# The output projection of a hybrid decoder block as seven quarter products

## The chip, the cores and the metric

The kernel runs on one core of one Trainium2 chip. The metric is the device time of one execution in microseconds.

## What is computed

One decoder layer on 512 tokens of width 1024. Cut to what matters here:

```python
merged = jax.nn.sigmoid(gate_a) * (ya @ w_branch_a[l]) + jax.nn.sigmoid(gate_b) * (yb @ w_branch_b[l])
h = h + merged @ w_out[l]                 # the output projection: 512x1024 by 1024x1024
xn2 = rms_norm(h, norm2_w[l])
h = h + (jax.nn.silu(xn2 @ w_ffn_gate[l]) * (xn2 @ w_ffn_up[l])) @ w_ffn_down[l]
```

## The kernel before, in words

Every product is formed from operands that are split in two: a high part (rounded to the matmul type by ScalarE, `w_hi`, `A_hi`, `mg_hi`) and the low rest (`x - high`, formed by VectorE or GpSimd, `w_lo`, `A_lo`, `mg_lo`). Each tile product is three matmuls: high by high, high by low, low by high.

The five engines run programs written out by hand, and semaphores order them; there is no scheduler. The stages in order of time: the input projection, the gated attention and gating unit, the *merge* (gates and branches, seven *pairs* of weight blocks), the output projection, the feed-forward *pairs* (gate and up) and the down projection.

In the merge and the feed-forward a pair is computed by a seven-product scheme for 2x2 blocks (Strassen-Winograd). With weight quarters A11, A12, A21, A22 the left operands are A11, A12, A22 and the sums S1 = A21 + A22, S2 = S1 - A11, S3 = A11 - A21, S4 = A12 - S2. The right operands are quarters of the activations and the differences T1 = x12 - x11, T2 = x22 - T1, T3 = x22 - x12, T4 = x21 - T2. Seven products of a quarter each give what eight plain ones would. There the weight sums lie in PSUM (`chain` in banks 4 and 5, `diff` in banks 6 and 7), and the products are collected in banks 0 to 3 (`product`, L2104).

The output projection before does not use this. `W_out` arrives in four blocks of two 128-row slices by 1024 columns (1 MB each, SyncE, L394 and L398). ScalarE rounds each (`out_high`, `high2`), VectorE (`low_out`, the first) or GpSimd (`low_out`, `low`) forms its low part. `block_N` (L1899) then runs, for each block, over four row tiles t, two halves of 512 columns and two slices k: 3 matmuls of 512 columns each, 48 in a block, 192 in all, with the merged rows as the stationary operand. The eight sums (4 row tiles, 2 halves) fill all eight PSUM banks. In the last block, while row tiles 2 and 3 are multiplied, row tiles 0 and 1 of h already go through `residual` (VectorE), `stats_h` and `normalise_h` (ScalarE) and are turned on TensorE (`turn`, 8 transposes) for the feed-forward.

What is merged is formed during and just after merge pair 7: GpSimd multiplies the branch products by the gates (`weighted(7)`, L508, two instructions, after the last quarter `merge_c12` of pair 7), VectorE adds the branches (`merged_sum(u)`, L1529, u = 0 to 3), ScalarE rounds (`merged_high`, L914), VectorE subtracts (`merged_low`, L1542).

## Time and profile before

| what | value |
|---|---|
| median of 3 runs | 817.0 us (816.84 to 817.6) |
| span of the profiled execution | 815.2 us |
| TensorE busy (matmul) | 808.4 us, 99% |
| VectorE, ScalarE, GpSimd busy | 539.7, 440.4, 414.0 us |
| from the last matmul of merge pair 7 to the first of the feed-forward | 424.7 to 470.3 us |

Of the profiled execution the profile gives the span, from the first to the last instruction; it has no further time of its own. "PE" is TensorE, "PEld" its weight load, "DVE" VectorE, "ACT" ScalarE, "POOL" GpSimd, "SP" SyncE. A duration behind a time is that of one instruction, or of x so many from the start of the first to the end of the last. Durations of instructions in a row overlap by a few hundredths, since the next starts while the last one drains.

### The profile page before, as it was taken

To read this page: it belongs to the slowest core of one execution; us is meant where nothing else is said; L and a number is where in the kernel's file an instruction comes from. 1 tells how busy PE (TensorE), PEld (TensorE's weight loads), DVE (VectorE), ACT (ScalarE), POOL (GpSimd) and SP (SyncE) were. 2 spreads that over 40 slices of the span, in tenths; PEclk is the share of its full clock that TensorE was granted. 3 is DMA by queue.
4 is the path that set the end of the run, shared out by engine and by line. 5 is a ranking of instruction groups with operands and counts; after the bars stand their busy time and mean duration, and the time that the engine had idled before them with its cause. 6 is when DMAs were issued, how large, how long until landed. Compare 5 with 4: busy or idle time off the path is not lost.

```text
span 815.2 us, 13365 instructions
## 1 busy us (share of the span) xinstructions
PE 808.4 (99%) x5504; PEld 750.1 (92%) x5504; DVE 539.7 (66%) x561; ACT 440.4 (54%) x501; POOL 414.0 (51%) x146
## 2 busy tenths in 40 slices
PE   9999999999999999999999999999999999999997
PEld 7888888888888899999998899999999999999985
DVE  5377377374674867888873278766667777677736
ACT  5523446665665645866542584454444446665624
POOL 4445424424224543477954543544444445978880
PEclk9999999999999999999999999999999999999999
DMA  7973523121123253322234203423234445535022
GB/s 294 265 263 115 164 95 104 52 104 57 52 98 115 95 204 105 104 104 105 103 130 185 104 1 107 152 106 109 106 111 159 159 152 186 178 125 212 1 78 104
DMA packets 27565, 103.11 MB, mean 126 GB/s; under 512 B 2816, under 2 KB 4224, under 8 KB 23552
## 3 DMA queue, kind: packets, MB, share of 16 engines
q1 hardware_dynamic: 22288, 87.07, 29.8%
q10 hardware_dynamic: 5232, 15.40, 5.9%
q8 instruction: 33, 0.54, 0.3%
...
## 4 chain that ended last, share of the span: by engine, by line
PE 99%; DMA 0%; ACT 0%; issue 0%; SPq 0%; DVE 0%; ACTq 0%
PE acc L2109 14%; PE acc L2112 14%; PE acc L2111 14%; PE acc L1894 7%; PE acc L1896 6%; PE acc L1895 6%; PE acc L1913 6%; PE acc L1912 6%; PE acc L1911 6%; PE acc L2308 3%; PE acc L2307 3%; PE acc L2305 3%; PE acc L1940 3%; PE acc L2023 1%; PE acc L2062 1%; PE acc L2067 1%
## 5 line engine op out<-in xcount | busy, mean ns | idle before, releaser
L465 POOL TENSOR_TENSOR w_lo<-raw,w_hi 128x2048 fp32r<-128x2048 f32 x26 | 123.1, 4733 | 163.1 <-ACT w_hi L660 163.1
L486 POOL TENSOR_TENSOR A_lo<-wp,A_hi 128x1024 fp32r<-128x1024 f32 x51 | 126.1, 2472 | 145.6 <-ACT A_hi L833 137.3
L848 ACT ACTIVATE S_hi<-acc 128x1024 fp32r<-128x1024 f32 x68 | 68.1, 1024 | 89.5 <-PE acc L2112 56.3
L2112 PE MATMUL acc<-xt_hi,A_lo 128*128 128x256 f32 x408 | 115.5, 283 | 0.0
L2111 PE MATMUL acc<-xt_lo,A_hi 128*128 128x256 f32 x408 | 115.5, 283 | 0.0
L2109 PE MATMUL acc<-xt_hi,A_hi 128*128 128x256 f32 x408 | 115.5, 283 | 0.0
L1444 DVE TENSOR_TENSOR S_lo<-acc,S_hi 128x1024 fp32r<-128x1024 f32 x68 | 81.8, 1220 | 18.6 <-ACT S_hi L848 18.6
L1894 PE MATMUL acc<-xt_hi,w_hi 128*128 128x512 f32 (+1 forms) x240 | 92.5, 385 | 0.0
L1896 PE MATMUL acc<-xt_hi,w_lo 128*128 128x512 f32 (+1 forms) x240 | 91.7, 382 | 0.0
L1895 PE MATMUL acc<-xt_lo,w_hi 128*128 128x512 f32 (+1 forms) x240 | 91.7, 382 | 0.0
L660 ACT ACTIVATE w_hi<-raw 128x2048 fp32r<-128x2048 f32 x26 | 49.5, 1909 | 64.1 <-PE acc L1913 43.3
L2111 PEld LDWEIGHTS acc<-xt_lo,A_hi 128*128 128x128 f32 x408 | 78.3, 192 | 0.0
L2109 PEld LDWEIGHTS acc<-xt_hi,A_hi 128*128 128x128 f32 x408 | 78.3, 192 | 0.0
L2112 PEld LDWEIGHTS acc<-xt_hi,A_lo 128*128 128x128 f32 x408 | 78.3, 192 | 0.0
L2109 PE MATMUL acc<-tb_hi,S_hi 128*128 128x256 f32 x240 | 67.9, 283 | 0.0
L2111 PE MATMUL acc<-tb_lo,S_hi 128*128 128x256 f32 x240 | 67.9, 283 | 0.0
L2112 PE MATMUL acc<-tb_hi,S_lo 128*128 128x256 f32 x240 | 67.9, 283 | 0.0
L833 ACT ACTIVATE A_hi<-wp 128x1024 fp32r<-128x1024 f32 x51 | 53.8, 1055 | 17.9 <-PE acc L2112 17.9
L1896 PEld LDWEIGHTS acc<-xt_hi,w_lo 128*128 128x128 f32 x240 | 45.1, 188 | 8.8
L1894 PEld LDWEIGHTS acc<-xt_hi,w_hi 128*128 128x128 f32 x240 | 45.1, 188 | 8.8
L1895 PEld LDWEIGHTS acc<-xt_lo,w_hi 128*128 128x128 f32 x240 | 45.1, 188 | 8.5
L2109 PE MATMUL acc<-mt_hi,S_hi 128*128 128x256 f32 x168 | 47.7, 284 | 0.0
...
## 6 DMA issues: line engine op xcount, KB each, us to landing
wp<-wstream SPq DMA_DIRECT2D x34, 1024.0 KB, 6.9
raw<-wstream SPq DMA_DIRECT2D x26, 1024.0 KB, 4.8
...
raw_out<-wstream SPq DMA_DIRECT2D x2, 1024.0 KB, 5.8
```

The lines of the kernel that those rows point to most:

```text
L465: pool.tensor_tensor(w_lo[s][:, :], raw[s][:, :], w_hi[s][:, :], ALU.subtract).then_inc(lo_ready, 1)
L486: pool.tensor_tensor(low_of(name, rows), weights_of(name, c, rows), high_of(name, rows), ALU.subtract).then_inc(plain_low, 1)
L660: a.activation(w_hi[s][:, :], raw[s][:, :], ACT.Copy).then_inc(hi_ready, 1)
L833: a.activation(high_of(name, rows), weights_of(name, c, rows), ACT.Copy).then_inc(op_high, 1)
L848: a.activation(high_of(name, rows), src, ACT.Copy).then_inc(op_high, 1)
L1444: v.tensor_tensor(low_of(name, rows), src, high_of(name, rows), ALU.subtract).then_inc(s_low, 1)
L1894: pe.matmul(dst, wh[:, k, cs], rh[:, k, ts], start=(k == 0), stop=False)
L1895: pe.matmul(dst, wh[:, k, cs], rl[:, k, ts], start=False, stop=False)
L1896: last = pe.matmul(dst, wl[:, k, cs], rh[:, k, ts], start=False, stop=(k == KD - 1))
L2109: pe.matmul(dst, wh[:, g, k, :], x[0][:, k, :], start=(start and g == 0 and k == 0), stop=False, skip_group_check=True)
L2111: pe.matmul(dst, wh[:, g, k, :], x[1][:, k, :], start=False, stop=False, skip_group_check=True)
L2112: mm = pe.matmul(dst, wl[:, g, k, :], x[0][:, k, :], start=False, stop=(k == 3), skip_group_check=True)
```

## The change

The output projection is computed by the same seven-product scheme, with quarters of 512 by 512 weights. A quarter product (`out_product`) runs over two row tiles and four slices with 3 matmuls of 512 columns: 24 matmuls, 168 in the seven. The merged rows (and their differences `mgt`, formed by VectorE) are the stationary operand. `W_out` comes in eight transfers of half a quarter (512 KB). The weight sums (`out_chain`, and S3 in the place of A21) lie in SBUF, because all eight banks hold products: A11 and A12 in 4 and 5, S1 and S4 in 6 and 7, S2 in 0 and 1, S3 and A22 in 2 and 3. What several quarters share goes through `out_u2` and `out_u3`; GpSimd adds it to three quarters of h (`based`), VectorE adds the rest from the banks (`residual`). Some semaphores elsewhere are joined into one; no other stage changes. Here and below "S1's low" is the low part of that operand.

```diff
-        raw_out = [sb(f"raw_out{s}", 120 + 16 * s, [P, BLK]) for s in range(2)]
-        raw_ffn = [sb(f"raw_ffn{s}", 181 + 8 * s, [P, BLK]) for s in range(2)]
+        out_raw = {n: sb(f"out_raw_{n}", kb, [P, 4, HALF]) for n, kb in (("A11", 112), ("A21", 120), ("A12", 128), ("A22", 136))}
+        out_chain = sb("out_chain", 32, [P, 4, HALF])
+        OUT_SLOT = {"A11": (16, 24), "S1": (0, 8), "S2": (181, 189), "S3": (16, 24), "A12": (0, 8), "A22": (181, 189), "S4": (197, 40)}
+        out_hi = {n: sb(f"out_{n}_hi", kb[0], [P, 4, HALF], F32R) for n, kb in OUT_SLOT.items()}
+        out_lo = {n: sb(f"out_{n}_lo", kb[1], [P, 4, HALF], F32R) for n, kb in OUT_SLOT.items()}
+        mgt = [sb(f"mgt{n}", 160 + 4 * n, [P, 4, HT]) for n in range(4)]
+        out_u2 = sb("out_u2", 104, [P, 2, HALF])
...
-            sp.wait_ge(t_formed, N_FORMED)
-            for s in range(2):
-                sp.dma_start(raw_out[s][:, :], wstream[W_OUT + s]).then_inc(raw_landed[s], 16)
-            sp.wait_ge(hi_ready, B_OUT + 2)
...
+            sp.wait_ge(t_low, N_LOW)
+            for name, landed in out_landed.items():
+                i, j = int(name[1]) - 1, int(name[2]) - 1
+                for n in range(2):
+                    sp.dma_start(out_raw[name][:, 2 * n:2 * n + 2, :],
+                                 wstream[W_OUT + 2 * j + n].rearrange("p (k n) -> p k n", k=2)[:, :, i * HALF:(i + 1) * HALF]
+                                 ).then_inc(landed, 16)
+            sp.wait_ge(out_low_pool, 1)
+            sp.wait_ge(out_formed, 3)
+            sp.dma_start(raw_ffn[0][:, :], wstream[W_FFN]).then_inc(ffn_landed[0], 16)
+            sp.wait_ge(out_low, 3)
+            sp.dma_start(raw_ffn[1][:, :], wstream[W_FFN + 1]).then_inc(ffn_landed[1], 16)
+            sp.wait_ge(out_done, 10)
...
-            low_out(1)
...
+            def based(n, ts, hs, u):
+                pool.wait_ge(out_joined, n)
+                pool.tensor_tensor(h[:, ts, hs], h[:, ts, hs], u[:, :, :], ALU.add).then_inc(h_based, 1)
+            out_low_of("A11", 1)
             weighted(MERGE_PAIRS)
-            for b in range(B_OUT + 2, B_FFN):
-                low(b, b % 2, 8 * (b - b % 2) + 16)
+            pool.wait_ge(mg_high, 4)
+            pool.tensor_tensor(xt_lo[:, 4:8, 0:HT], sg_a[:, 4:8, 0:HT], xt_hi[:, 4:8, 0:HT], ALU.subtract).then_inc(mg_low_pool, 1)
+            pool.wait_ge(mg_high, 5)
+            pool.tensor_tensor(mt_lo[2][:, :, :], mgt[2][:, :, :], mt_hi[2][:, :, :], ALU.subtract).then_inc(mg_low_pool, 1)
+            out_low_of("A12", 5)
+            pool.wait_ge(h_landed, 16)
+            based(2, slice(2, 4), slice(HALF, D), out_u3)
+            based(1, slice(0, 2), slice(HALF, D), out_u2)
+            based(1, slice(2, 4), slice(0, HALF), out_u2)
...
+            pool.wait_ge(out_low, 5)
             ffn_low(0)
...
+                if p == MERGE_PAIRS:
+                    a.wait_ge(plain_low, 3 * p - 3)
+                    a.wait_ge(s_formed, 4 * p - 4)
+                    out_high_of("A11", out_raw["A11"])
...
+                    merged_high(xt_hi[:, 0:4, 0:HT], sg_a[:, 0:4, 0:HT], msum=2)
...
+                    merged_high(mt_hi[0][:, :, :], mgt[0][:, :, :], formed=1)
...
-            a.wait_ge(product_done, 7 * MERGE_PAIRS)
-            a.dma_start(h[:, :, :], x.rearrange("(t p) n -> p t n", p=P)).then_inc(h_landed, 16)
+            a.wait_ge(plain_low, 3 * MERGE_PAIRS)
+            a.wait_ge(s_formed, 4 * MERGE_PAIRS)
+            out_high_of("S1", out_chain, 1)
+            a.wait_ge(product_done, 7 * MERGE_PAIRS - 1)
+            out_high_of("S2", out_chain, 2)
             a.wait_ge(joined, 5 * MERGE_PAIRS)
             a.dma_start(ident[:, :], ident_d).then_inc(ident_landed, 16)
-            merged_high(2)
-            merged_high(3)
+            a.wait_ge(out_done, 2)
+            a.wait_ge(branch_taken, 8)
+            a.activation(out_u2[:, :, :], acc[:, 4:6, :], ACT.Copy).then_inc(out_taken, 1)
+            out_high_of("S3", out_raw["A21"], 3)
+            merged_high(mt_hi[1][:, :, :], mgt[1][:, :, :], formed=2)
+            merged_high(xt_hi[:, 4:8, 0:HT], sg_a[:, 4:8, 0:HT], msum=4)
+            merged_high(mt_hi[2][:, :, :], mgt[2][:, :, :], formed=3)
+            a.wait_ge(out_done, 4)
+            out_high_of("A12", out_raw["A12"])
+            merged_high(xt_hi[:, 0:4, HT:SEQ], mgt[3][:, :, :], formed=4)
+            merged_high(xt_hi[:, 4:8, HT:SEQ], sg_a[:, 4:8, HT:SEQ], msum=4)
+            a.wait_ge(out_done, 6)
+            a.dma_start(h[:, :, :], x.rearrange("(t p) n -> p t n", p=P)).then_inc(h_landed, 16)
+            out_high_of("A22", out_raw["A22"])
+            out_high_of("S4", out_chain, 4)
...
-            for j in range(2):
-                high2(B_OUT + 2 + j, j % 2, block_used, 6 + j + 1)
-            a.wait_ge(block_used, 6 + 3)
+            a.wait_ge(out_done, 8)
             ffn_high(0)
+            ffn_high(1)
...
                     merged_sum(1)
-                    merged_low(0)
-                    low_out()
+                    v.wait_ge(msum_ready, 2)
+                    mgt_form(0, m12, m11)
+                    merged_low(xt_lo[:, 0:4, 0:HT], m11, xt_hi[:, 0:4, 0:HT], 1)
+                    v.wait_ge(out_landed["A21"], OUT_LANDED)
+                    v.wait_ge(out_landed["A22"], OUT_LANDED)
+                    v.tensor_tensor(out_chain[:, :, :], out_raw["A21"][:, :, :], out_raw["A22"][:, :, :], ALU.add).then_inc(out_formed, 1)
+                    merged_low(mt_lo[0][:, :, :], mgt[0][:, :, :], mt_hi[0][:, :, :], 2)
...
             merge_c12(MERGE_PAIRS)
-            merged_low(1)
-            for u in (2, 3):
-                merged_sum(u)
-                merged_low(u)
...
+            out_low_of("S1", out_chain, 2)
+            v.wait_ge(out_low, 1)
+            v.tensor_tensor(out_chain[:, :, :], out_chain[:, :, :], out_raw["A11"][:, :, :], ALU.subtract).then_inc(out_formed, 1)
+            v.tensor_tensor(out_raw["A21"][:, :, :], out_raw["A11"][:, :, :], out_raw["A21"][:, :, :], ALU.subtract).then_inc(out_formed, 1)
+            merged_sum(2)
+            out_low_of("S2", out_chain, 3)
+            merged_sum(3)
+            v.wait_ge(msum_ready, 4)
+            mgt_form(1, m22, mgt[0][:, :, :])
+            mgt_form(2, m22, m12)
+            merged_low(mt_lo[1][:, :, :], mgt[1][:, :, :], mt_hi[1][:, :, :], 3)
+            out_low_of("S3", out_raw["A21"], 4)
+            v.wait_ge(mgt_formed, 2)
+            mgt_form(3, m21, mgt[1][:, :, :])
+            v.wait_ge(out_low, 2)
+            v.wait_ge(out_landed["A12"], OUT_LANDED)
+            v.tensor_tensor(out_chain[:, :, :], out_raw["A12"][:, :, :], out_chain[:, :, :], ALU.subtract).then_inc(out_formed, 1)
+            merged_low(xt_lo[:, 0:4, HT:SEQ], mgt[3][:, :, :], xt_hi[:, 0:4, HT:SEQ], 6)
+            merged_low(xt_lo[:, 4:8, HT:SEQ], m22, xt_hi[:, 4:8, HT:SEQ], 7)
+            v.wait_ge(out_done, 6)
+            v.wait_ge(out_taken, 1)
+            v.tensor_tensor(out_u2[:, :, :], acc[:, 0:2, :], out_u2[:, :, :], ALU.add).then_inc(out_joined, 1)
+            out_low_of("A22", out_raw["A22"], 6)
+            v.wait_ge(out_done, 8)
+            v.wait_ge(out_joined, 1)
+            v.tensor_tensor(out_u3[:, :, :], acc[:, 2:4, :], out_u2[:, :, :], ALU.add).then_inc(out_joined, 1)
+            out_low_of("S4", out_chain, 7)
+            def residual(t, hf, b, done):
+                v.wait_ge(out_done, done)
+                hs = h[:, t, hf * HALF:(hf + 1) * HALF]
+                v.tensor_tensor(hs, bank[b][:, :], hs, ALU.add).then_inc(h_joined, 1)
             v.wait_ge(h_landed, 16)
+            residual(0, 0, 4, 9)
+            residual(1, 0, 5, 10)
+            v.wait_ge(h_based, 1)
+            residual(2, 1, 6, 4)
+            residual(3, 1, 7, 4)
+            v.wait_ge(h_based, 2)
...
-            residual(0, 16)
+            residual(0, 1, 2, 11)
             rstd_h(0)
-            residual(1, 16)
+            residual(1, 1, 3, 12)
             rstd_h(1)
             weigh_turned(0)
-            residual(2, 16)
...
-                block_N(j % 2, mg_hi[:, ks, :], mg_lo[:, ks, :], j == 0, j == 3, quarters_taken, turn_h)
...
+            def out_product(name, x, b, start, between=None):
+                wh, wl = out_hi[name], out_lo[name]
+                for t in range(2):
+                    dst = bank[b + t][:, :]
+                    ts = slice(t * P, (t + 1) * P)
+                    for k in range(4):
+                        pe.matmul(dst, x[0][:, k, ts], wh[:, k, :], start=(start and k == 0), stop=False, skip_group_check=True)
+                        pe.matmul(dst, x[0][:, k, ts], wl[:, k, :], start=False, stop=False, skip_group_check=True)
+                        mm = pe.matmul(dst, x[1][:, k, ts], wh[:, k, :], start=False, stop=(k == 3), skip_group_check=True)
+                        if between is not None and k == 1:
+                            between(t)
+                    mm.then_inc(out_done, 1)
+            pe.wait_ge(out_low_pool, 1)
+            pe.wait_ge(mg_low, 1)
+            out_product("A11", x11, 4, True)
+            pe.wait_ge(out_low, 1)
+            pe.wait_ge(mg_low, 2)
+            out_product("S1", mt1, 6, True)
+            pe.wait_ge(taken, 2 * MERGE_PAIRS)
+            pe.wait_ge(joined, 5 * MERGE_PAIRS)
+            pe.wait_ge(out_low, 2)
+            pe.wait_ge(mg_low, 3)
+            out_product("S2", mt2, 0, True)
+            pe.wait_ge(out_low, 3)
+            pe.wait_ge(mg_low_pool, 2)
+            out_product("S3", mt3, 2, True)
+            pe.wait_ge(out_taken, 1)
+            pe.wait_ge(out_low_pool, 2)
+            out_product("A12", x21, 4, False)
+            pe.wait_ge(out_low, 4)
+            pe.wait_ge(mg_low, 4)
+            pe.wait_ge(out_joined, 2)
+            out_product("A22", t4, 2, False)
+            def turn_h(t):
+                turn(hn[:, t, :], 2 * t, t)
+            pe.wait_ge(out_low, 5)
+            pe.wait_ge(mg_low, 5)
+            pe.wait_ge(h_joined, 4)
+            pe.wait_ge(ident_landed, 32)
+            out_product("S4", x22, 6, False, turn_h)
```

On VectorE, before, from the last two quarters of merge pair 7 on (`sg_a`, `sg_b` hold the two gated branches, `mcq` the quarters of the pair, `mg` the merged rows, `w_lo0` the first block's low part; brackets name semaphores waited for):

```order
L1535 TENSOR_TENSOR w_lo0_53<-raw_out0_112,w_hi0_51 128x2048 [waits product_done,hi_ready]
L1507 TENSOR_TENSOR mcq_72<-acc,mu2_74 128x512 [waits product_done] x2
L1542 TENSOR_TENSOR mg_lo_94<-sg_a_97,mg_hi_93 128x1024 [waits mg_hi_ready]
L1529 TENSOR_TENSOR sg_a_97<-sg_a_97,sg_b_98 128x1024 [waits branch_taken]
L1542 TENSOR_TENSOR mg_lo_94<-sg_a_97,mg_hi_93 128x1024 [waits lo_ready,mg_hi_ready]
```

and with the change, from the same two quarters to the low part of T2 (`mt_lo1`), the last operand that product S2 waits for:

```order
L1544 TENSOR_TENSOR mcq_72<-acc,mu2_74 128x512 [waits product_done] x2
L1579 TENSOR_TENSOR out_S1_lo_123<-out_chain_114,out_S1_hi_116 128x2048 [waits out_high]
L1647 TENSOR_TENSOR out_chain_114<-out_chain_114,out_raw_A11_110 128x2048 [waits out_low]
L1648 TENSOR_TENSOR out_raw_A21_111<-out_raw_A11_110,out_raw_A21_111 128x2048
L1566 TENSOR_TENSOR sg_a_95<-sg_a_95,sg_b_96 128x1024 [waits branch_taken]
L1579 TENSOR_TENSOR out_S2_lo_124<-out_chain_114,out_S2_hi_117 128x2048 [waits out_high]
L1566 TENSOR_TENSOR sg_a_95<-sg_a_95,sg_b_96 128x1024 [waits branch_taken]
L1571 TENSOR_TENSOR mgt1_130<-sg_a_95,mgt0_129 128x1024 [waits msum_ready]
L1571 TENSOR_TENSOR mgt2_131<-sg_a_95 128x1024
L1575 TENSOR_TENSOR mt_lo1_69<-mgt1_130,mt_hi1_66 128x1024 [waits mg_high]
```

Before, one low part (L1542) stood between the last quarter and the second block of weights. Now nine instructions stand between the last quarter and product S2, and all of them read two operands in SBUF.

On GpSimd, before, from the low part of A22 of merge pair 7 on:

```order
L486 TENSOR_TENSOR A_lo<-wp_127,A_hi 128x1024 [waits op_high]
L608 TENSOR_TENSOR w_lo_54<-raw_out_113,w_hi_52 128x2048 [waits hi_ready,lo_ready,product_done]
L508 TENSOR_TENSOR sg_b<-mcq,sg_b 128x1024 [waits joined,taken,tile_free,gates_taken]
L508 TENSOR_TENSOR sg_b<-mcq,sg_b 128x1024
L465 TENSOR_TENSOR w_lo_53<-raw_49,w_hi_51 128x2048 [waits hi_ready,raw_landed0]
```

and with the change:

```order
L498 TENSOR_TENSOR A_lo<-wp_148,A_hi 128x1024 [waits op_high]
L620 TENSOR_TENSOR out_A_lo<-out_raw_A_110,out_A_hi 128x2048 [waits out_high]
L520 TENSOR_TENSOR sg_b<-mcq,sg_b 128x1024 [waits joined,taken,tile_free,gates_taken]
L520 TENSOR_TENSOR sg_b<-mcq,sg_b 128x1024
L631 TENSOR_TENSOR xt_lo<-sg_a,xt_hi 128x4x256 [waits mg_high]
L633 TENSOR_TENSOR mt_lo_70<-mgt_131,mt_hi_67 128x1024 [waits mg_high]
L620 TENSOR_TENSOR out_A_lo<-out_raw_A_112,out_A_hi 128x2048 [waits out_high]
L626 TENSOR_TENSOR h<-h,out_u_134 128x2x512 [waits out_joined,h_landed]
L626 TENSOR_TENSOR h<-h,out_u_133 128x2x512 [waits out_joined] x2
L642 TENSOR_TENSOR w_lo_53<-raw_ffn_135,w_hi_51 128x2048 [waits hi_ready,out_low]
```

The low part of A11 no longer waits for VectorE and the pair's fifth product (`lo_ready`, `product_done`), so it runs right behind A22's; and three additions into h are new.

## Rows read from the trace of the kernel before

**Rows 1.** The page: busy time, and the chain that ended last by engine

```profile
PE 808.4 (99%) x5504; PEld 750.1 (92%) x5504; DVE 539.7 (66%) x561; ACT 440.4 (54%) x501; POOL 414.0 (51%) x146
...
PE 99%; DMA 0%; ACT 0%; issue 0%; SPq 0%; DVE 0%; ACTq 0%
```

**Rows 2.** Windows: merge pair 7, the output projection (PEclk: granted clock, 1.00 full)

```profile
core 0: us, PE busy (x) PEld busy (x) DVE busy (x) ACT busy (x) POOL busy (x), PEclk, DMA share, GB/s
404.60:424.70 20.10, 20.10 (x170) 20.10 (x169) 14.34 (x14) 10.02 (x10) 11.01 (x5) 1.00 0.34 130
424.70:470.30 45.60, 45.60 (x212) 37.92 (x212) 17.90 (x19) 16.81 (x21) 25.20 (x8) 1.00 0.41 156
```

**Rows 3.** Chain of waits (start us, us, what), and the turns in the last block

```profile
424.94 0.23 PE acc L1911
...
464.41 0.87 PE acc L1883 x8
...
468.03 0.87 PE acc L1883 x8
...
470.29 3.83 PE acc L2211 x32
```

**Rows 4.** Timeline of VectorE (start us, us, what, idle before), 414 to 435 us

```profile
414.52 1.22 DVE L1444 TENSOR_TENSOR S_lo<-acc,S_hi 128x1024 fp32r<-128x1024 f32 x1 [0.37 <-ACT S_hi L848]
415.66 1.22 DVE L1529 TENSOR_TENSOR sg_a<-sg_a,sg_b 128x1024 f32<-128x1024 f32 x1
416.79 0.68 DVE L1504 TENSOR_TENSOR u<-acc,mu 128x512 f32<-128x512 f32 x1
...
420.45 2.28 DVE L1535 TENSOR_TENSOR w_lo<-raw_out,w_hi 128x2048 fp32r<-128x2048 f32 x1
...
424.98 0.69 DVE L1507 TENSOR_TENSOR mcq<-acc,mu 128x512 f32<-128x512 f32 x1 [1.64 <-PE acc L2112]
425.59 3.33 DVE L1542 TENSOR_TENSOR mg_lo<-sg_a,mg_hi 128x1024 fp32r<-128x1024 f32 x1
431.20 3.41 DVE L1529 TENSOR_TENSOR sg_a<-sg_a,sg_b 128x1024 f32<-128x1024 f32 x1 [2.28 <-POOL sg_b L508]
```

**Rows 5.** Timeline of GpSimd over the same stretch

```profile
412.04 2.41 POOL L486 TENSOR_TENSOR A_lo<-wp,A_hi 128x1024 fp32r<-128x1024 f32 x1
423.23 4.61 POOL L608 TENSOR_TENSOR w_lo<-raw_out,w_hi 128x2048 fp32r<-128x2048 f32 x1 [8.78 <-DVE w_lo L1535]
427.80 5.72 POOL L508 TENSOR_TENSOR sg_b<-mcq,sg_b 128x1024 f32<-128x1024 f32 x2
```

**Rows 6.** Timelines of both engines from 371 us

```profile
371.79 3.02 DVE L1487 TENSOR_TENSOR yb<-yb,rt_b 128x1024 f32<-128x1024 f32 x1 [2.05 <-POOL xt_lo L512]
...
375.34 1.21 DVE L1444 TENSOR_TENSOR S_lo<-acc,S_hi 128x1024 fp32r<-128x1024 f32 x1
...
371.33 2.40 POOL L486 TENSOR_TENSOR A_lo<-wp,A_hi 128x1024 fp32r<-128x1024 f32 x1
373.69 5.77 POOL L508 TENSOR_TENSOR sg_a<-mcq,sg_a 128x1024 f32<-128x1024 f32 x2
```

**Rows 7.** Timelines of both engines from 266 us

```profile
269.35 5.73 DVE L1420 TENSOR_TENSOR yb<-yb,rs 128x512 f32<-128x512 f32 x2
...
266.95 7.58 POOL L481 TENSOR_TENSOR mt_lo<-mt_raw,mt_hi 128x1024 fp32r<-128x1024 f32 x3 [4.57 <-ACT mt_hi L824]
```

**Rows 8.** Timeline of ScalarE from 414 us

```profile
414.38 1.90 ACT L918 ACTIVATE w_hi<-raw_out 128x2048 fp32r<-128x2048 f32 x1
...
434.64 1.06 ACT L914 ACTIVATE mg_hi<-sg_a 128x1024 fp32r<-128x1024 f32 x1 [13.44 <-DVE sg_a L1529]
```

**Rows 9.** DMA issues (KB each, us to landing), 395 to 460 us, and SyncE's first issue

```profile
raw_out<-wstream SPq DMA_DIRECT2D x2, 1024.0 KB, 5.8
...
h<-x ACTq DMA_DIRECT2D x1, 2048.0 KB, 13.6
...
400.91 0.82 SPq L394 DMA_DIRECT2D raw_out<-wstream  x2
```

**Rows 10.** Timelines of VectorE and ScalarE: row tile 0 of h to its normalised rows

```profile
460.36 0.69 DVE L1613 TENSOR_TENSOR h<-acc,h 128x512 f32<-128x512 f32 x1 [0.60 <-PE acc L1913]
...
461.09 1.06 ACT L673 ACTIVATE sq_junk<-h 128x1024 f32<-128x1024 f32 x1
...
462.80 1.34 ACT L1000 ACTIVATE hn<-h,small 128x512 f32<-128x512 f32 x2 [0.23 <-DVE small L1619]
```

**Rows 11.** Groups by line, shapes apart: the one wait of TensorE over 0.4 us

```profile
L1930 PE MATMUL acc<-ones_dv 128*128 128x128 f32 x20 | 4.1, 386 | 1.2 <-DVE ones_dv L1203 1.2
```

More of the change, by code:

```diff
@@ L256, in build @@
         hi_ready, lo_ready, block_used = sem("hi_ready"), sem("lo_ready"), sem("block_used")
-        x_landed = [sem(f"x_landed{t}") for t in range(TT)]
+        rows_landed = [sem(f"rows_landed{t}") for t in range(TT)]
         xt_landed = [None] + [sem(f"xt_landed{q}") for q in range(1, 4)]
@@ L1619, in rstd_h @@
                 v.reciprocal(rstd[:, t:t + 1], sd[:, t:t + 1]).then_inc(rstd_ready, 1)
-            residual(0, 16)
+            residual(0, 1, 2, 11)
             rstd_h(0)
-            residual(1, 16)
+            residual(1, 1, 3, 12)
             rstd_h(1)
             weigh_turned(0)
-            residual(2, 16)
+            v.wait_ge(h_based, 3)
+            residual(2, 0, 6, 13)
             weigh_turned(1)
@@ L1629, in _ @@
             rstd_h(2)
-            residual(3, 16)
+            residual(3, 0, 7, 14)
             rstd_h(3)
```

193 lines of the change are left out of this document (81 added, 112 removed).

## The prediction

> **What bounds the kernel now.** I read the page first, then the windows, then the timelines of the three helper engines around the output projection. TensorE is busy for 99% of the span and makes 99% of the chain that ended last [rows 1]. So a matmul that goes away gains its time, and a wait that comes in costs its whole length. In the windows TensorE has no gap in merge pair 7 (20.10 us) nor in the output projection (45.60 us), and VectorE is busy for 17.90, GpSimd for 25.20 us of the latter [rows 2]. What the reader is to look for in the timelines is when each operand becomes ready, and how long VectorE and GpSimd take when both work at once.
>
> **What is removed.** From the first matmul of the old stage to the feed-forward it is 45.60 us [rows 2], and two turns of 0.87 us are in it [rows 3]. That leaves 43.86 us for 192 matmuls, 0.228 us each (the chain shows 0.23). The new stage has 168 of the same form: one quarter product takes 24 x 0.228 = 5.48 us, and the gain before any wait is the same 24 matmuls, **-5.5 us**.
>
> **The price of a helper's instruction.** On VectorE 1024 elements take 1.22 us and 2048 take 2.28 us [rows 4]; on GpSimd 2.41 and 4.61 us [rows 5]; on ScalarE 1.06 and 1.90 us [rows 8]. That holds when an engine works alone. At 425.59 VectorE's low part, both inputs in SBUF, took 3.33 us and ended at 428.92, which is 1.08 us behind the end of GpSimd's L608 (423.23 + 4.61 = 427.84). At 431.20 it took 3.41 us and ended at 434.61, again 1.09 us behind GpSimd (427.80 + 5.72 = 433.52). GpSimd in its turn took 5.72 us for two where twice 2.41 is 4.82 [rows 4, 5]. The same earlier: VectorE ends at 374.81, 1.08 us behind GpSimd's 373.73, and the next two on GpSimd take 5.77 us. But its low part with an input in PSUM (L1444, 375.34) takes 1.21 us in the midst of them [rows 6]. So an instruction of VectorE with both inputs in SBUF and one of GpSimd never run together: the one that asks later waits for the other's end. Two instructions of VectorE with little work took 5.73 us against three of GpSimd (7.58 us) [rows 7]: when both have more to do, they take turns. The old weight sums lie in PSUM and escape this. The new ones do not.
>
> No row shows an instruction of 2048 elements on VectorE waiting so. Below, it could overlap in part; above, it could pay 2.28 behind GpSimd's end. I take 2.14, from 2.28 less the 0.14 by which 1.08 is below 1.22. The Trainium skill ("SBUF — State Buffer", section "Who interferes with whom") says that a VectorE instruction with two SBUF inputs and a GpSimd one that reads SBUF exclude each other for the whole instruction; it names no size, and by that rule the sum below stands as it is.
>
> **The new chain, step by step** (times are those of the old trace, carried on; TensorE leaves merge pair 7 at 424.78).
>
> 1. *Merge pair 7.* GpSimd forms A11's low part right behind A22's, 414.4 to 419.0. `merged_sum(0)`, asked for at 415.66 [rows 4], ends at 420.05 instead of 416.88. u3, one quarter, `merged_sum(1)` and T1 follow, to 423.6, then the low part of x11, to 424.76. Product A11 can start at 424.8: no wait, but the margin is gone. The cover of all this was VectorE's idle time in pair 7 (5.8 of 20.1 us [rows 2]).
> 2. *S1.* The sum A21 + A22 to 426.95, T1's low to 428.1, two quarters to 429.3 (the last one at 425.7 before [rows 4]), S1's low to 431.5. Product A11 ends at 430.3. **Wait 1.2 us.**
> 3. *S2.* Behind S1's low VectorE and GpSimd take turns: GpSimd's first gated product to 433.7, S2's sum to 435.9, the second gated product to 438.15, S3's sum to 440.3. Then VectorE alone: merged sum 441.4, S2's low 443.6, merged sum 444.7, T2 446.0, T3 447.1, T2's low 448.3. Product S1 ends at 437.0. **Wait 11.4 us.** It is the largest term: nine instructions of VectorE from 429.2 on (four of 2.28 and five of 1.22, 15.2 us), and 4.5 us of GpSimd between them, less 0.6 that neighbours overlap, is 19.1 us to 448.3, against two products of 5.48.
> 4. *S3.* S3's low waits for x21's low on GpSimd (to 450.6) and ends at 452.7; then T3's low on GpSimd, to 455.0. Product S2 ends at 453.8. **Wait 1.2 us.**
> 5. *A12.* GpSimd's low part, behind T4 on VectorE, ends at 460.55; product S3 at 460.5. **Wait 0.1 us.**
> 6. *A22.* VectorE, behind that: S4's sum 462.7, low parts of T4 and x22 465.0, u2 466.1, A22's low 468.3, u3 469.4. Product A12 ends at 466.1. **Wait 3.4 us.**
> 7. *S4.* It needs banks 6 and 7 free: u3, then S4's low (471.6), then GpSimd's first addition into h (473.9), then two residuals (475.2). Product A22 ends at 474.9. **Wait 0.3 us.** h itself is asked for at 458 here. It took 13.6 us to land before, with 2 MB of other weights beside it [rows 9]; at 472 it would still be in time for GpSimd, give or take 0.3.
> 8. *The first turn.* GpSimd's second addition ends at 476.2, the residual at 476.9. From there to normalised rows it took 3.1 us (461.05 to 464.14) [rows 10], so 480.0; TensorE is at the turn at 476.6. **Wait 3.4 us.** The second turn and the feed-forward lie as far behind it as before.
>
> ScalarE costs nothing: it has its high parts ready 0.5 us or more before VectorE asks, except for T1, T2 and T4, whose steps are in the chain. The quarters of W_out are asked for at 400.9, as before, and a 1 MB transfer took 5.8 us [rows 9]; A11 is wanted at 408.2, A21 and A22 at 424.7, four times 1 MB. If A11 landed as late as 414.5 (13.6 us), its low part and the merged sums behind it would slip, and the sum would rise by 2 to 3 us; that goes into the range. The joined semaphores and the other order of the feed-forward's first weights cost nothing: GpSimd's low part for block 0 ends at 483 to 484, behind three additions, and the feed-forward asks at 486.
>
> **The sum.** 1.2 + 11.4 + 1.2 + 0.1 + 3.4 + 0.3 + 3.4 = 21.0 us of waits, less 5.5, is **+15.5 us**, rounded up by 0.1 for the handovers. On the profiled span of 815.2 us that is 830.8; the runs' median lies 1.8 us above that span, so 817.0 + 15.6 = **832.6 us**.
>
> **Rivals.**
>
> *The clock falls.* The windows show full clock, 1.00, that is 2.4 GHz [rows 2], and the page has before it no idle time of TensorE over 1.2 us, at the start of the kernel [rows 11]. What 11.4 us of idle time does, no row shows. At 1.2 GHz a matmul of 0.228 would take 0.456 us, a whole quarter product 5.5 us more. Behind the wait of step 3 that is hidden: product S3 and A12 would end at 464.8 and 470.3, A22 would start 0.9 late, and step 8 would swallow it. Behind the waits of steps 6 and 8 it would not: half to a whole product at 1.2 GHz gives 2.7 to 5.5 us, 835.3 to 838.1 us. The Trainium skill ("TensorE: Matmul & The Clock Gate", Part 1) has the clock drop to half when TensorE has been idle, and come back under work; by that rule the long wait surely drops it, and the short ones may. Chance 0.22.
>
> *The exclusion is weaker in the new shapes* (large instructions, strided quarters), so that only some of them wait: about half of what it adds, 825 us. Chance 0.14.
>
> *No exclusion there at all.* Then the last quarter ends at 426.1, and T2's low at 440.8: nine instructions of VectorE still don't fit under the 11 us of products A11 and S1. Wait 5.1 us before S2 and none after: 5.1 - 5.5 gives -0.4, 816.6 us. Against it speak four places of the trace [rows 4 to 6]. Chance 0.08, half of it within 0.2%, half faster.
>
> *Faster.* The operands are in time: it decides whether T2's low is ready when product S1 ends, 437.0 or 435.7 without step 2. Were VectorE to get there, everything behind it would have 5 us more for the same work, and the 24 matmuls are gained: 811.5 us. It needs that the sums take no more than half of what they are priced at above, for instance if W_out's sums were formed well inside merge pair 7; the order of the program has S2's and S3's sums behind the last quarter, which speaks against it. Chance 0.05.
>
> **How the numbers follow.** A measurement of this kernel can tell about 0.2% (1.6 us) from no change. Forecast 0.51, clock 0.22, weak exclusion 0.14, no exclusion 0.08, faster 0.05 make 1. Slower: 0.51 + 0.22 + 0.14, and 0.01 for no exclusion with a late transfer, 0.88. Within 0.2%: 0.04. Faster: 0.08. The range reaches from 822, below the weak exclusion (0.14) by 3 us for its own uncertainty, to 838, where the clock's rival ends; what is left out is no exclusion, faster, and some 0.06 above.
>
> **What would show each step.** In the timelines: L1566 at 415.7 lasting over 4 us behind GpSimd's L620 (step 1); TensorE idle before `out_product` S2 for 11 us, ended by VectorE's `mt_lo` (step 3); VectorE's instructions of 2048 elements lasting 4.4 us beside GpSimd's (steps 3, 4, 6), alone 2.28; idle time of 3 us before A22, ended by `out_u`, and before the first turn, ended by ScalarE's `hn`. PEclk below 1.00 in the windows behind the waits would show the first rival. The prediction is wrong if VectorE's instructions with two SBUF inputs keep 1.22 and 2.28 us beside a busy GpSimd, or if product S2 starts before 445.

## The result, and the profile after

The changed kernel takes **836.9 us** (median of 4 runs, 835.4 to 837.5) against 817.3 us (816.8 to 817.6) on the same chip: a ratio of 1.0238, 95% interval 1.0224 to 1.0253. It is slower by 19.6 us; the forecast was 832.6 us, in a range of 822 to 838. The profiled execution spans 834.1 us, 18.9 more than that of before.

The page after, busy times and the chain that ended last:

```profile
PE 809.2 (97%) x5480; PEld 749.2 (90%) x5480; DVE 582.2 (70%) x576; ACT 449.9 (54%) x508; POOL 428.8 (51%) x150
...
PE 93%; DVE 5%; issue 1%; ACT 1%; POOL 0%; DVEq 0%; ACTq 0%; POOLq 0%
```

TensorE's part of the chain fell from 99% [rows 1] to 93%, and VectorE has taken 5%. TensorE is busy for as long as before, though it has 24 matmuls less; the clock, below, is most of the reason. Every wait of TensorE between 402 and 500 us (engine, tile and line <- what ended it: us in total, times, longest):

```profile
PE acc L2261 <- DVE mt_lo L1575: 11.0, 1, 11.0
PE acc L2261 <- DVE out_u L1671: 2.3, 1, 2.3
PE acc L2321 <- DVE xt_lo L1265: 2.2, 1, 2.2
PE acc L2181 <- DVE u L1541: 1.7, 1, 1.7
PE acc L1955 <- ACT hn L1040: 1.2, 1, 1.2
```

The two L2261 are the products S2 and A22, L2321 is the feed-forward's second block, L2181 is product A22 of merge pair 7, L1955 the first turn. Where before there was none of these, there are now 18.4 us. The window of the stage in the same kernel (columns as in [rows 2]):

```profile
427.40:486.60 59.20, 44.65 (x186) 35.64 (x185) 52.57 (x36) 29.72 (x30) 36.63 (x11) 0.86 0.30 108
```

From its first product to the first matmul of the feed-forward the stage took 45.34 us before (424.78 to 470.12) and takes 59.23 now (427.38 to 486.61). VectorE is busy for 52.57 us of it, where it had 17.90 [rows 2]. The account: 24 matmuls less, -5.45; waits, 59.20 - 44.65 = 14.55; and TensorE is busy for 4.8 us more than 168 matmuls at 0.227 us and two turns of 0.87 us need (44.7 against 39.9). Together +13.9. Pair 7 itself takes 22.07 instead of 20.16 us (+1.9), the feed-forward's second block comes 2.4 us later still, and 0.7 us were lost at the very start of the kernel, where the experiments below, all alike up to there, differ by as much among themselves. That is 18.9.

VectorE after (start us, us, what):

```profile
416.35 4.46 DVE L1566 TENSOR_TENSOR sg_a<-sg_a,sg_b 128x1024 f32<-128x1024 f32 x1
...
430.18 2.29 DVE L1579 TENSOR_TENSOR out_S_lo<-out_chain,out_S_hi 128x2048 fp32r<-128x2048 f32 x1
432.50 4.36 DVE L1647 TENSOR_TENSOR out_chain<-out_chain,out_raw_A 128x2048 f32<-128x2048 f32 x1
436.79 4.47 DVE L1648 TENSOR_TENSOR out_raw_A<-out_raw_A,out_raw_A 128x2048 f32<-128x2048 f32 x1
...
449.26 4.48 DVE L1579 TENSOR_TENSOR out_S_lo<-out_raw_A,out_S_hi 128x2048 fp32r<-128x2048 f32 x1
453.66 3.41 DVE L1571 TENSOR_TENSOR mgt<-sg_a,mgt 128x1024 f32<-128x1024 f32 x1
456.99 6.72 DVE L1661 TENSOR_TENSOR out_chain<-out_raw_A,out_chain 128x2048 f32<-128x2048 f32 x1
...
486.39 6.25 DVE L1265 TENSOR_TENSOR xt_lo<-hx,xt_hi 128x512 fp32r<-128x512 f32 x2
```

GpSimd after:

```profile
415.11 4.61 POOL L620 TENSOR_TENSOR out_A_lo<-out_raw_A,out_A_hi 128x2048 fp32r<-128x2048 f32 x1
430.50 8.61 POOL L520 TENSOR_TENSOR sg_b<-mcq,sg_b 128x1024 f32<-128x1024 f32 x2 [10.78 <-DVE mcq L1544]
449.11 2.48 POOL L631 TENSOR_TENSOR xt_lo<-sg_a,xt_hi 128x1024 fp32r<-128x1024 f32 x1 [9.99 <-ACT xt_hi L936]
451.56 4.43 POOL L633 TENSOR_TENSOR mt_lo<-mgt,mt_hi 128x1024 fp32r<-128x1024 f32 x1
455.95 5.61 POOL L620 TENSOR_TENSOR out_A_lo<-out_raw_A,out_A_hi 128x2048 fp32r<-128x2048 f32 x1
470.60 9.00 POOL L626 TENSOR_TENSOR h<-h,out_u 128x1024 f32<-128x1024 f32 x3 [9.04 <-DVE out_u L1671]
...
487.08 5.01 POOL L642 TENSOR_TENSOR w_lo<-raw_ffn,w_hi 128x2048 fp32r<-128x2048 f32 x1
```

This is the rule of [rows 4 to 6], now with 2048 elements. The instruction of 2048 elements that takes 2.28 us alone takes 4.36 to 4.48 beside GpSimd. The S4 sum at 456.99 is asked for behind A12's low part and takes 6.72 us: it ends at 463.71, 2.15 us behind GpSimd's end (455.95 + 5.61 = 461.56). The forecast had taken 2.14. Two gated products on GpSimd take 8.61 where they took 5.72 [rows 5]: the first, at 430.50, finds VectorE in S1's low part (430.18, 2.29 us), and VectorE's S2 sum runs between the two.

TensorE after, at the start of products S2 and A22:

```profile
449.49 0.77 PE L2261 MATMUL acc<-out_S_hi,mt_hi 128*128 128x512 f32 x1 [11.04 <-DVE mt_lo L1575]
450.05 0.63 PE L2262 MATMUL acc<-out_S_lo,mt_hi 128*128 128x512 f32 x1
...
454.31 0.40 PE L2263 MATMUL acc<-out_S_hi,mt_lo 128*128 128x512 f32 x1
...
470.60 0.47 PE L2261 MATMUL acc<-out_A_hi,xt_hi 128*128 128x512 f32 x1 [2.29 <-DVE out_u L1671]
470.91 0.39 PE L2262 MATMUL acc<-out_A_lo,xt_hi 128*128 128x512 f32 x1
471.14 0.45 PE L2263 MATMUL acc<-out_A_hi,xt_lo 128*128 128x512 f32 x1
471.38 0.63 PE L2261 MATMUL acc<-out_A_hi,xt_hi 128*128 128x512 f32 x1
...
474.78 0.39 PE L2263 MATMUL acc<-out_A_hi,xt_lo 128*128 128x512 f32 x1
```

Behind the 11 us wait the matmuls follow one another in 0.43 us (the first in 0.56) until 454.3, then in 0.23: eleven matmuls, 4.82 us for what takes 2.5 at full clock. Behind the 2.3 us wait it is the same, but the slow stretch begins only with the third or fourth matmul, while TensorE is busy. Two windows, over S2's start and within A22, name the granted clock (last but two):

```profile
450.00:458.00 8.00, 8.00 (x28) 6.35 (x27) 8.00 (x3) 2.68 (x2) 8.00 (x3) 0.73 0.39 133
...
472.00:474.00 2.00, 2.00 (x7) 1.51 (x6) 1.85 (x3) 0.00 (x0) 2.00 (x1) 0.50 0.91 352
```

0.50 is the 1.2 GHz level. So the first rival, that the clock falls, happened as well as the forecast. What it costs is the question of the fourth run below; the second and the third bear on it too.

### The profile page after: what moved, and what is told of

It is laid out like the page before. It is cut to its first block, busy times and chain, and to the rows that moved or that the text cites. A ratio compares the mean times of both kernels' runs of the same rounds, so it can differ in the third digit from the quotient of the medians.

```text
span 834.1 us, 13353 instructions
## 1 busy us (share of the span) xinstructions
PE 809.2 (97%) x5480; PEld 749.2 (90%) x5480; DVE 582.2 (70%) x576; ACT 449.9 (54%) x508; POOL 428.8 (51%) x150
## 4 chain that ended last, share of the span: by engine, by line
PE 93%; DVE 5%; issue 1%; ACT 1%; POOL 0%; DVEq 0%; ACTq 0%; POOLq 0%
PE acc L2181 13%; PE acc L2184 13%; PE acc L2183 13%; PE acc L1966 6%; PE acc L1968 6%; PE acc L1967 6%; PE acc L1985 4%; PE acc L1984 4%; PE acc L1983 4%; PE acc L2409 3%; PE acc L2412 3%; PE acc L2411 3%; PE acc L2012 3%; DVE sg_a L1566 1%; PE acc L2261 1%
## 5 line engine op out<-in xcount | busy, mean ns | idle before, releaser
L477 POOL TENSOR_TENSOR w_lo<-raw,w_hi 128x2048 fp32r<-128x2048 f32 x24 | 113.3, 4720 | 153.3 <-ACT w_hi L685 153.2
L2181 PE MATMUL acc<-xt_hi,A_hi 128*128 128x256 f32 x408 | 115.5, 283 | 1.7 <-DVE u L1541 1.7
L873 ACT ACTIVATE S_hi<-acc 128x1024 fp32r<-128x1024 f32 x68 | 68.1, 1024 | 89.5 <-PE acc L2184 56.3
L2181 PEld LDWEIGHTS acc<-xt_hi,A_hi 128*128 128x128 f32 x408 | 78.3, 192 | 1.9 <-issue 1.9
L685 ACT ACTIVATE w_hi<-raw 128x2048 fp32r<-128x2048 f32 x24 | 45.8, 1911 | 58.6 <-PE acc L1985 38.4
L2181 PE MATMUL acc<-tb_hi,S_hi 128*128 128x256 f32 x240 | 67.9, 283 | 0.0
L2181 PE MATMUL acc<-mt_hi,S_hi 128*128 128x256 f32 x168 | 47.7, 284 | 0.0
```

The source lines that it names most:

```text
L477: pool.tensor_tensor(w_lo[s][:, :], raw[s][:, :], w_hi[s][:, :], ALU.subtract).then_inc(lo_ready, 1)
L685: a.activation(w_hi[s][:, :], raw[s][:, :], ACT.Copy).then_inc(hi_ready, 1)
L873: a.activation(high_of(name, rows), src, ACT.Copy).then_inc(op_high, 1)
L2181: pe.matmul(dst, wh[:, g, k, :], x[0][:, k, :], start=(start and g == 0 and k == 0), stop=False, skip_group_check=True)
```

## The experiments

Theory A, in all of them: the time is set by the queues of VectorE and GpSimd, which exclude each other when VectorE has two SBUF inputs; TensorE only waits for them. The rivals are named with each. The kernel before ran with each series again (medians of 817.0 to 817.5 us). The changed kernel did not: its 836.9 us, with which the runs below are compared, is the result above, and its four runs lie up to 2.2 us apart. What a run gained is therefore given from the profiled spans too, where the parts can be named. The stage's length is counted from the first product to the feed-forward, 59.23 us in the changed kernel.

### The feed-forward's low part, later

```diff
             pool.wait_ge(out_done, 14)
+            pool.wait_ge(xt_ready, 4 + 2)
             ffn_low(1)
```

> The changed kernel with one wait more: GpSimd's low part of the second feed-forward block waits until VectorE has formed the low part of row tile 1 (two instructions with both inputs in SBUF). Theory A (the two engines exclude each other, and this place was missed in the forecast): VectorE's two instructions take 1.3 to 1.5 us instead of 6.25, the wait of TensorE at 492.8 (2.2 us) goes, and the time falls by 2.2 us, from 836.9 to about 834.7. Theory B (VectorE is late there for a reason of its own, its long queue): 6.25 us stay about as long, and the time stays at 836.9, or rises, since GpSimd starts later.

Measured: 833.03 us, ratio 1.0183 (1.0157 to 1.0208), span 831.3. The 2.2 us wait before the feed-forward's second block is gone; the stage is 59.22 us, unchanged. VectorE:

```profile
486.02 1.91 DVE L1266 TENSOR_TENSOR xt_lo<-hx,xt_hi 128x512 fp32r<-128x512 f32 x2
```

What follows: the small low part of the turned activations (L1265) had lain behind a 5 us low part on GpSimd; 6.25 us became 1.91. The profiled span fell by 2.8 us (2.4 of them in the feed-forward, 0.3 at the start of the kernel), the median by 3.9, where 2.2 had been expected.

### GpSimd only writes

Left out of the computation: the nine instructions of GpSimd in the output projection write constants in place of low parts, gated products and additions. One of the places of the edit:

```diff
-                pool.tensor_tensor(out_lo[name][:, :, :], out_raw[name][:, :, :], out_hi[name][:, :, :], ALU.subtract
-                                   ).then_inc(out_low_pool, 1)
+                pool.memset(out_lo[name][:, :, :].bitcast(F32), 0.0).then_inc(out_low_pool, 1)
```

> The changed kernel, in which GpSimd's nine instructions of the stage (low parts of A11, A12, x21 and T3, the two gated products of pair 7, three additions into h) are each a memset of the same destination behind the same waits; that part of the computation is left out. Theory A (exclusion is what costs): a memset reads nothing, so VectorE's instructions keep 1.22 and 2.28 us next to it; the wait before S2 falls from 11.0 to about 5, the waits before A22 and before the first turn go, and the time falls by 13 to 15 us, to 822 to 824 (GpSimd's low part for the second feed-forward block is left as it is and still costs its 2.2). Theory B (VectorE's own queue is what is too long): VectorE ends as late as before but for GpSimd's shorter durations on its chain (two gated products), the wait before S2 stays at 8 us or more, and the time falls by 3 us or less.

Measured: 822.12 us, ratio 1.0054 (1.0042 to 1.0067), span 820.3; the stage 48.07 us. TensorE's waits:

```profile
PE acc L2263 <- DVE mt_lo L1577: 5.4, 1, 5.4
PE acc L2323 <- DVE xt_lo L1267: 1.8, 1, 1.8
```

VectorE in this run:

```profile
426.56 2.28 DVE L1581 TENSOR_TENSOR out_S_lo<-out_chain,out_S_hi 128x2048 fp32r<-128x2048 f32 x1
...
441.36 2.28 DVE L1581 TENSOR_TENSOR out_S_lo<-out_raw_A,out_S_hi 128x2048 fp32r<-128x2048 f32 x1
```

and GpSimd, whose writes of constants run beside both (S2's sum, 2.29 us from 428.87 on, has GpSimd idle by then):

```profile
426.84 1.86 POOL L521 MEMSET sg_b<- 128x1024 f32 x2 [10.32 <-DVE mcq L1546]
441.19 0.95 POOL L633 MEMSET xt_lo<- 128x1024 f32 x1 [12.49 <-ACT xt_hi L938]
...
443.94 1.81 POOL L623 MEMSET out_A_lo<- 128x2048 f32 x1 [0.85 <-ACT out_A_hi L945]
```

What follows: 14.8 of the 19.6 us go with these nine instructions. Two things went at once, GpSimd's own time (0.95 instead of 2.41 us for 1024 elements) and the time for which VectorE stood; this run does not tell them apart; the last three bear on that. (The Trainium skill, "SBUF — State Buffer", section "Who interferes with whom", has a GpSimd instruction that only writes SBUF leave VectorE alone. By that rule this run frees VectorE in the whole stage, and its durations of 2.28 us here agree.) The 5.4 us before S2 that are left are VectorE's own queue: the forecast's rival "no exclusion" had 5.1. Behind them TensorE waits for nothing up to the feed-forward, but the clock had fallen: products S2 and S3 take 13.44 us (441.59 to 455.03) where 48 matmuls need 10.9, so the slow clock costs 2.5 us of this run's time. The granted clock from 440 to 450 us is 0.66, and 1.00 in the stretches before and after.

### Only A11's low part replaced

Left out: the low part of A11 is zero.

```diff
-            out_low_of("A11", 1)
+            pool.wait_ge(out_high, 1)
+            pool.memset(out_lo["A11"][:, :, :].bitcast(F32), 0.0).then_inc(out_low_pool, 1)
             weighted(MERGE_PAIRS)
```

> The changed kernel, in which only GpSimd's low part of A11, next to merge pair 7, is a memset (A11's low part is left out). Theory A: VectorE's merged sum at 416.4 takes 1.22 instead of 4.46 us, TensorE's 1.7 us of waiting inside pair 7 go, and all behind it is 3.2 us earlier: 836.9 falls to about 833.7. Theory B (the 3.2 us are taken up again by slack further on, since what counts is the wait for the gated products): 836.9 falls by less than 1 us.

Measured: 833.64 us, ratio 1.0195 (1.0164 to 1.0225), span 831.8; the stage 57.91 us, and pair 7's 1.7 us wait is gone. VectorE:

```profile
415.84 1.22 DVE L1567 TENSOR_TENSOR sg_a<-sg_a,sg_b 128x1024 f32<-128x1024 f32 x1
```

What follows: one instruction of GpSimd in a stage that TensorE seemed to bound costs 3.2 us of the median, 2.3 of the span. The merged sum takes 1.22 instead of 4.46 us, u3 follows it 3 us sooner, and S2 waits 9.7 us. From the start of pair 7 to the feed-forward 3.2 us are gained (78.06 for 81.30); behind the 2.2 us wait of the feed-forward's second block the clock then falls, which it did not do in the changed kernel's profile, and takes 1.5 us back.

### TensorE kept busy through the wait before S2

```diff
+            for _ in range(84):
+                pe.matmul(bank[0][:, 0:HT], xt_hi[:, 0, 0:P], xt_hi[:, 0, 0:HT], start=True, stop=True, skip_group_check=True)
             pe.wait_ge(out_low, 2)
             pe.wait_ge(mg_low, 3)
             out_product("S2", mt2, 0, True)
```

> The changed kernel with 84 matmuls of 256 columns (about 10 us) into bank 0 ahead of product S2, which overwrites them: TensorE has work in the long wait and should keep its clock. Theory A (the slow clock behind the wait is hidden, since S3 to the first turn wait for VectorE and GpSimd): matmuls of S2 are 0.228 us apart instead of 0.43, the granted clock of 450 to 458 us is 1.00, and the time stays within 0.5 us of 836.9. Theory C (the clock is what cost more than forecast): the time falls by 2.4 us or more.

Measured: 836.67 us, ratio 1.0223 (1.0192 to 1.0255), span 834.9. The stage: 59.23 us (426.67 to 485.90), to the hundredth as without the fillers. The window of the old wait (the granted clock, 1.00, is last but two):

```profile
440.00:446.00 6.00, 6.00 (x53) 6.00 (x52) 5.96 (x5) 1.92 (x1) 0.00 (x0) 1.00 0.54 175
```

and its waits. The first was 2.3 us, the second is what the fillers left of the 11.0, the third had not been there:

```profile
PE acc L2261 <- DVE out_u L1671: 3.2, 1, 3.2
...
PE acc L2261 <- DVE mt_lo L1575: 1.0, 1, 1.0
PE acc L2261 <- POOL mt_lo L633: 0.9, 1, 0.9
```

What follows: S2 ran at full clock, and the 2.3 us came back as a wait before S3 (0.9) and a longer one before A22 (3.2 for 2.3). Behind that one A22 ran slower (8.32 us for 7.14), and the 1.2 us wait before the first turn was gone in its turn: the turn comes where it comes in the changed kernel, 53.1 us behind the stage's first product. The clock behind the long wait is paid out of waits that would be there anyway.

### S2's operands before S3's

ScalarE rounds S3 correspondingly later (not in the cut).

```diff
-            v.tensor_tensor(out_raw["A21"][:, :, :], out_raw["A11"][:, :, :], out_raw["A21"][:, :, :], ALU.subtract).then_inc(out_formed, 1)
...
-            mgt_form(2, m22, m12)
             merged_low(mt_lo[1][:, :, :], mgt[1][:, :, :], mt_hi[1][:, :, :], 3)
+            v.tensor_tensor(out_raw["A21"][:, :, :], out_raw["A11"][:, :, :], out_raw["A21"][:, :, :], ALU.subtract).then_inc(out_formed, 1)
+            mgt_form(2, m22, m12)
```

> The changed kernel in another order: on VectorE the sum for S3 and the difference T3, which product S2 does not need, come behind T2's low part instead of ahead of S2's operands, and ScalarE rounds S3 later. Theory A (what counts is the whole work of VectorE and GpSimd, which exclude each other; the wait before S2 is only where it shows first): the wait before S2 falls from 11.0 to 8 to 9 us, but the waits before S3 and A22 grow by as much or more, and the time stays at 836.9 or rises, by up to 2 us. Theory D (the wait before S2 is the cost, and behind it VectorE has time to spare): the time falls by 2 to 3 us, to 834 to 835.

Measured: 838.60 us, ratio 1.0265 (1.0248 to 1.0282), span 836.7; the stage 62.81 us. The first two of its waits:

```profile
PE acc L2261 <- DVE mt_lo L1575: 8.8, 1, 8.8
PE acc L2261 <- POOL mt_lo L633: 2.6, 1, 2.6
```

What follows: the longest wait shrank by 2.2 us and the kernel did not gain. T3's low part on GpSimd now comes last (asked for at 454.11, 3.50 us), S3 waits 2.6 for it, and everything behind is later. Of the 3.6 us by which the stage grew, 1.4 are the clock, which fell behind the first turn's wait (2.4 us): the twelve matmuls behind that turn take 4.26 us for 2.85. So the run shows that there is nothing to gain in this order, and not how much the order loses.

### The additions into h almost empty

Left out: GpSimd adds only 8 of 512 columns into h.

```diff
-                pool.tensor_tensor(h[:, ts, hs], h[:, ts, hs], u[:, :, :], ALU.add).then_inc(h_based, 1)
+                pool.tensor_tensor(h[:, ts, hs.start:hs.start + 8], h[:, ts, hs.start:hs.start + 8], u[:, :, 0:8], ALU.add).then_inc(h_based, 1)
```

> The changed kernel in which GpSimd's three additions into h take 8 columns of each row tile instead of 512, so that most of what they add is left out. Theory A: the waits before the first turn (1.2 us) and, in part, the 6.8 us of GpSimd's work on the chain of h go: the first turn comes some 2.3 us earlier, and 836.9 falls to about 834.6. Theory D: the additions lie beside TensorE's work, and the time stays within 0.5 us.

Measured: 833.34 us, ratio 1.0205 (1.0188 to 1.0222), span 831.3; the stage 57.47 us (-1.8). The wait for `hn` before the first turn is gone, the others stand within 0.5 us. Of the 2.8 us by which the span fell, 1.8 are the stage and 0.7 the start of the kernel. So the step at the stage's end is right in kind: these additions are the last link before the turn.

### Low parts moved from GpSimd to VectorE

Two runs. In the first the low parts of A11 and A12 go to VectorE, with the later low part of the first experiment; in the second those of x21 and T3 too. Nothing is left out.

```diff
-            out_low_of("A11", 1)
             weighted(MERGE_PAIRS)
...
+                if last:
+                    plain_out_low("A11", 1)
                 merge_u2(p)
...
             out_low_of("S3", out_raw["A21"], 4)
+            plain_out_low("A12", 5)
```

> The changed kernel, repaired in part, all of the computation in it: the low parts of A11 (now in VectorE's idle time in merge pair 7) and A12 are formed by VectorE in 2.3 us each instead of GpSimd's 4.6, and GpSimd's low part for the second feed-forward block waits as in the first experiment. Theory A (two engines that exclude each other are one engine, and GpSimd is its slow half): the 9.2 us of GpSimd's become 4.6 on VectorE; with the 2.2 to 3.9 us of the first experiment the time falls to 828 to 830. Theory B (VectorE's own queue is too long): VectorE gets 4.6 us more to do, and the time is that of the first experiment, 833.0, or above.

> The kernel of the run before this with the low parts of x21 and T3 on VectorE too (1.2 us each instead of 2.4 on GpSimd), each right ahead of the product that needs it. Theory A: another 2.4 us of exclusive time go, the time falls by about 2 us, to 826 to 828, and stays above the 817.3 of the kernel before. Theory B: no gain over the run before, or a loss of 2 us.

Measured: 829.16 us, ratio 1.0150 (1.0133 to 1.0167), and 826.37 us, ratio 1.0115 (1.0098 to 1.0132). The stage 56.43 and 54.32 us. VectorE in the second: A11's low part beside GpSimd's gated product of an earlier pair, S2's sum beside those of pair 7 (S3's sum, behind it, takes 4.50), S3's low part with GpSimd idle:

```profile
410.33 4.12 DVE L1578 TENSOR_TENSOR out_A_lo<-out_raw_A,out_A_hi 128x2048 fp32r<-128x2048 f32 x1
...
429.49 4.37 DVE L1648 TENSOR_TENSOR out_chain<-out_chain,out_raw_A 128x2048 f32<-128x2048 f32 x1
...
446.28 2.28 DVE L1574 TENSOR_TENSOR out_S_lo<-out_raw_A,out_S_hi 128x2048 fp32r<-128x2048 f32 x1
```

What follows: giving the busier engine more work made the kernel faster, twice. On VectorE the four low parts are 7.0 us of work (2.28, 1.22, 1.22, 2.28) and take 8.8, because A11's finds GpSimd at work and stands for 1.8, in what was VectorE's idle time. On GpSimd, in the changed kernel, they had made VectorE's instructions at 416.35, 449.26, 453.66 and 456.99 stand for 3.2, 2.2, 2.2 and 4.4 us, 12.0 in all. 10.5 us before S2 remain; the two sums are still beside GpSimd's gated products.

### The gated products too

Besides the gated products, S3's sum and T3 move behind T2's low part here, as they do in "S2's operands before S3's" (not in the cut).

```diff
-            weighted(MERGE_PAIRS)
...
+            for gp in range(2):
+                half_tiles = sg_b[:, 4 + 2 * gp:6 + 2 * gp, :].rearrange("p a (h t) -> p (a h) t", h=2)
+                v.tensor_tensor(half_tiles, mcq[:, :, gp, :], half_tiles, ALU.mult).then_inc(branch_taken, 1)
             merged_sum(2)
```

> The kernel of the run before it (low parts of the output projection on VectorE), and now also pair 7's two gated products on VectorE instead of GpSimd, with S3's sum and T3 behind T2's low part. GpSimd then does nothing between merge pair 7 and the additions into h. Theory A (the exclusion, and behind it VectorE's own queue): S2's and S1-side sums take 2.28 us instead of 4.37 and 4.50, the gated products 1.22 each instead of 4.1; T2's low part ends near 441.7 instead of 446.3 and TensorE's wait before S2 falls from 10.5 to 5 to 6 us. VectorE's work up to u3 shrinks by only about 2 us, so part of the 4.8 comes back as waits before S3 to A22: 822.5 to 825 us, still 5 us or more above the kernel before, since six sums and low parts of VectorE alone don't fit under the products A11 and S1. Rival (GpSimd's two instructions were not in the way; the order and the handovers to ScalarE set the time): the wait before S2 stays at 9 us or more and the time at 826 to 829. Rival that the scheme can win in this form: 817 or less.

Measured: 824.83 us, ratio 1.0094 (1.0077 to 1.0111), span 823.1; the stage 53.11 us. TensorE's waits:

```profile
PE acc L2272 <- DVE mt_lo L1569: 5.0, 1, 5.0
PE acc L2272 <- DVE out_u L1682: 1.9, 1, 1.9
PE acc L1966 <- ACT hn L1034: 1.2, 1, 1.2
```

and VectorE, with the sum and the gated products:

```profile
429.41 2.29 DVE L1647 TENSOR_TENSOR out_chain<-out_chain,out_raw_A 128x2048 f32<-128x2048 f32 x1
431.62 2.35 DVE L1654 TENSOR_TENSOR sg_b<-mcq,sg_b 128x1024 f32<-128x1024 f32 x2
```

What follows: the wait before S2 halved, to 5.0 us (how much of that is the gated products and how much the order, this run does not say), and only 1.2 us of the 5.5 arrived at the stage's end. VectorE has been busy almost without a gap since 414, its u3 for A22 comes at 461.9 (463.1 in the run before), and TensorE, sooner there, waits for it again. This is the fastest form tried, and it is still 7.8 us slower than the kernel before. None of the nine beats it. A form with the sums made inside merge pair 7, or in PSUM, was not tried.

## Why the prediction was right

The sum held where it was made: pair 7 and the output projection together came out 15.8 us longer, forecast 15.6. Its terms came out less well than the sum: 16.2 us of waits where 21.0 were forecast, and 5.0 us of slower TensorE work where none was. The two make up for each other because VectorE's and GpSimd's chain sets the end, and a TensorE that comes later finds a shorter wait; that is the mechanism of the forecast, and the slow clock in it is that of its first rival. The median is 4.3 us above the forecast: 2.4 from the feed-forward's second block, 0.7 from the start of the kernel, 1.0 because the runs' median lies 2.8 us above the profiled span and not 1.8, and 0.2 from the stages' sum. (The other three runs, with spans of 833.6, 835.0 and 835.3 us, lie 1.7 to 1.8 above their own; the profiled one lies 3.4 above, which nothing here explains.)

- *Price of a helper's instruction.* Right. 4.36 to 4.48 us were measured for 2048 elements beside GpSimd, 4.4 forecast. The rivals "weaker exclusion" and "no exclusion" are out; the second run makes the latter's case by force and lands at 822.1, not at its 816.6, since two things that this rival had let go remain: the feed-forward's second block (2.1, of them 1.8 the wait) and the slow clock behind the 5.4 us (2.5).
- *Step 1, merge pair 7.* "No wait, but the margin is gone" was wrong. Product A22 of pair 7 waits for u3, which stands behind the merged sum: 1.7 us. In its place S1's wait (1.2) vanished, since TensorE came 1.9 us later. The third run, without A11's low part, has no wait in pair 7.
- *Step 3, S2.* 11.4 forecast, 11.0 measured; the product starts at 449.49, and 448.3 was forecast, 449.0 with the 0.7 us from the start of the kernel.
- *Steps 4 and 5, S3 and A12.* 1.2 and 0.1 forecast, none measured: S2's own matmuls ran at half clock for 11 of 24 and filled that wait. With full clock (fourth run) 0.9 us stand before S3.
- *Steps 6 to 8.* 3.4, 0.3 and 3.4 forecast, 2.3, 0 and 1.2 measured. The times at which the helpers are ready were right within 1.1 us, 0.7 of them from the start of the kernel (u3 469.4 forecast, 470.5 measured; `hn` 480.0 and 480.5); the difference is TensorE, which arrived later for the slow clock. h took 8.4 us to land, not 13.6 [rows 9], and nobody waited for it. Nor was W_out late: 7.6 us for each half quarter.
- *"The second turn and the feed-forward lie as far behind it as before", and "the other order of the feed-forward's first weights cost nothing".* This is the step that failed. GpSimd's low part for block 1 now starts at 487.08, in the middle of VectorE's two low parts of the turned activations, and the exclusion that the forecast had priced everywhere else applies here as well: 6.25 us where VectorE before needed 1.47 (the row below this list). TensorE waits 2.2 us. The one wait more on GpSimd took back 3.9 us of the median and 2.8 of the span.
- *The clock.* It fell, and behind S2 it was hidden, as the rival's text had it. It fell behind A22's wait as well, where the rival had foreseen 2.7 to 5.5 us unhidden. That was also hidden, because the helpers' chain to the first turn (u3, the additions into h, `hn`) was later than TensorE by 1.2 us even so. Where a wait has no helper's chain behind it, the clock does cost: 2.5 us in the second run, and 1.5 us in the third and in the fourth, where it fell behind the wait of the feed-forward's second block (the rows below). In the changed kernel's profile it did not fall there. Whether it did in its runs with spans of 835.0 and 835.3 us stays open.

"Slower" had 0.88 of the chances, the forecast's own case 0.51.

VectorE's timeline in the kernel before, the two low parts of the step that failed:

```profile
469.89 1.47 DVE L1228 TENSOR_TENSOR xt_lo<-hx,xt_hi 128x512 fp32r<-128x512 f32 x2
```

TensorE behind the wait of the feed-forward's second block, in the third run and in the fourth; the same sixteen matmuls take 2.15 us in the changed kernel:

```profile
489.05 3.66 PE L2322 MATMUL acc<-xt_lo,w_hi 128*128 128x256 f32 x16 [2.19 <-DVE xt_lo L1266]
...
492.08 3.12 PE L2323 MATMUL acc<-xt_lo,w_hi 128*128 128x256 f32 x16 [2.17 <-DVE xt_lo L1265]
```
